# Moving the second output unit's split behind the scan, and the gate copy one head later

## The chip, the cores and the metric

The kernel is one program on one core of a Trainium2 chip. It works in float32 on a sequence of 256 tokens of width 1024. The metric is the device time of one execution in microseconds; of several executions the median is taken.

The engines named below are TensorE (PE in the profile, with PEld for its weight loads), VectorE (DVE), ScalarE (ACT), GpSimd (POOL) and SyncE (SP), whose queue issues the weight transfers.

## What is computed

The reference chains two blocks: two transformer layers, then a hybrid block of two gated MLPs with a mixer between them. The change lies in the mixer, which runs a latent attention (8 heads) and a state-space scan (16 heads) over one input projection and multiplies both results by one output matrix:

```python
def hybrid_mixer(h, positions, w_in, ...):
    proj = h @ w_in
    z, xs, Bm, Cm, dt_raw, cq, ckv, k_rope_raw = jnp.split(proj, IN_SPLITS, axis=-1)
    ...
    y = ssd_chunked(xh, dt, A, Bm, Cm)
    y = y + d_skip * xh
    yg = (y.reshape(b, S, D_SSD) * jax.nn.silu(z)).reshape(b, S, SSD_GROUPS, D_SSD // SSD_GROUPS)
    y_ssd = rmsnorm(yg, ssd_norm_w)
    ...
    attn = mla_causal_attention(q_nope, q_rope, k_nope, k_rope, v)
    y_mla = rmsnorm(attn, mla_norm_w)
    return jnp.concatenate([y_ssd, y_mla], axis=-1) @ w_out
```

## The kernel before

**Weight units.** All weights come in units of 1 MB (128 x 2048 numbers), through a ring of three slots. A unit takes three steps. SP loads it into `raw` (line 421 issues it). ACT copies it, rounded to the matmul's number format, into `whi` (line 593). DVE subtracts, `wlo = raw - whi` (line 1039). These two steps together are "the split" of a unit, and PE then multiplies by both parts, three matmuls for each product. Units are split strictly in order: `splits(n)` on ACT and on DVE does all units up to n that are still to do, and `w_hi`, `w_lo` and `w_used` count what ACT, DVE and PE have done. Three rules tie the ring together:

- SP loads unit n once DVE has split unit n - 3.
- ACT splits unit n once it has landed and PE has used unit n - 3.
- PE starts unit n once DVE has split it.

**The place.** The mixer's last input units are U_Z to U_Z+3, which give the gate z; its output units are U_OUT to U_OUT+7. U_OUT to U_OUT+3 multiply the latent attention's result (`bh`, `bl`), and U_OUT+4 to U_OUT+7 the scan's (`ah`, `al`). The order of everything is written out by hand, one in-order program for each engine. Around the change it is:

1. Split of U_OUT on ACT and on DVE.
2. The 8 latent heads (`mla_heads` on each engine). For head h PE computes the scores (`mla_score`, lines 2034, 2035 and 2020). DVE takes the row maximum (`head_max`, lines 1134, 1135 and 1138). ACT takes the exponential (`head_exp`, lines 716 and 718). PE transposes the weights (`weights_T`, line 1911). ACT copies them out of PSUM (`p_copy`, line 725). PE multiplies by the values (`values`, lines 1928 to 1930). PE's order in the loop is transposes of head h, scores of head h+2, values of head h-1.
3. The scan's preparation, and its 16 heads: PE lines 2336 to 2359, ACT lines 988 and 989, DVE line 1713.
4. `splits(U_OUT + 2)`, the silu of the second half of z, the sums y (lines 1706 and 1707), their norm (lines 1052 to 1058 and 1731), and `splits(U_OUT + 4)`. PE meanwhile runs U_OUT to U_OUT+2, then transposes the normed sums (line 1881), then runs U_OUT+3 and the rest.

**Inside step 2**, three pieces stand on DVE between the maxima that are no part of the heads. Behind head 1's maximum come the split of U_OUT+1 and the copy of half of z out of PSUM (line 1199; it waits on `z_half`, which PE signals ahead of the first transposes, and PE's values of heads 4 and on wait for it, since they reuse its two banks). Behind head 3's maximum comes `gate_diag` (line 1446). On ACT the split of U_OUT+1 stands between the exponential of head 1 and the copy of head 0's transposed weights.

Of the kernel before, what the change touches and what calls it, by code (L numbers as in the profile page):

```python
# [64 lines left out]
U_OUT = U_Z + 4  # L65
# [43 lines left out]
def build(nc, t_in, out):  # L109
    g = t_in  # L110
    with ExitStack() as ctx:
# [239 lines left out]
        def slot(n):  # L351
            return n % RING
# [4 lines left out]
        def bank(b, n=512):  # L357
            return ps[:, b, 0:n]
# [31 lines left out]
        def unit_size(n):  # L390
            if U_TAIL <= n < U_TAIL + 4:
                return 2 * TAILW
            if n == U_UQ + 1:
                return 768
            if n in (U_UQ, *U_KV):
                return 2 * 768
            return UNIT
# [186 lines left out]
        def _(act):  # L584
# [3 lines left out]
            def split(n, s, size=UNIT):  # L588

                act.wait_ge(w_landed[s], landed(n, s))  # L590
                if not isinstance(n, int) or n >= RING:
                    act.wait_ge(w_used, used(n))
                A.activation(whi[:, s, 0:size], raw[:, s, 0:size], ACT.Copy).then_inc(w_hi, 1)  # L593
# [13 lines left out]
            def splits(upto):  # L607
                while done[0] <= upto:
                    split(done[0], slot(done[0]), unit_size(done[0]))
                    done[0] += 1  # L610
# [100 lines left out]
            def head_exp(hg, h, src, scale):  # L711
                act.wait_ge(maxed, hg + 1)
                if h >= 2:
                    act.wait_ge(p_tr, hg - 1)
                b = h % 2
                A.activation(pb[:, b, 0:P], src(b)[:, 0:P], ACT.Exp, bias=nmx[:, b, 0:1], scale=scale,  # L716
                             accum_out=rs[:, 0, h:h + 1])
                A.activation(pb[:, b, P:SEG], src(b)[:, P:SEG], ACT.Exp, bias=nmx[:, b, 1:2], scale=scale,
                             accum_out=rs[:, 1, h:h + 1]).then_inc(exped, 1)

            def p_copy(hg, h):
                act.wait_ge(p_tr, hg + 1)
                if h >= 2:
                    act.wait_ge(pv_done, hg - 1)
                A.activation(pt[:, h % 2], bank(2 + h % 2, SEG), ACT.Copy).then_inc(p_copied, 1)
# [7 lines left out]
            def mla_heads(h0, scale):  # L733
                for h in range(HM):
                    head_exp(h0 + h, h, lambda b: bank(b, SEG), scale)
                    if h == 1:
                        splits(U_OUT + 1)
                    if h:
                        p_copy(h0 + h - 1, h - 1)
                p_copy(h0 + HM - 1, HM - 1)  # L740
# [224 lines left out]
            ins.then_inc(mqk_copied, 1)  # L965
            splits(U_OUT)
            mla_heads(2 * H, QK ** -0.5)

            for k, (lo, hi) in enumerate(O_PARTS):
# [52 lines left out]
        def _(dve):  # L1022
# [10 lines left out]
            def split(u, s, size=UNIT):  # L1033

                if isinstance(u, int):
                    dve.wait_ge(w_hi, u + 1)
                else:
                    dve.wait_ge(w_hi, u[1] * 6 + (u[0] + 1))
                V.tensor_tensor(wlo[:, s, 0:size], raw[:, s, 0:size], whi[:, s, 0:size].bitcast(F32),  # L1039
                                ALU.subtract).then_inc(w_lo, 1)  # L1040

            def splits(upto):
                while done[0] <= upto:
                    split(done[0], slot(done[0]), unit_size(done[0]))
                    done[0] += 1
# [85 lines left out]
            def head_max(hg, h, src, scale):  # L1131

                b = h % 2
                V.reduce_max(mx[:, b, 0:1], src[:, 0:P], AX_X)
                link(V.reduce_max(mx[:, b, 1:2], src[:, P:SEG], AX_X))
                if h >= 2:
                    dve.wait_ge(exped, hg - 1)
                V.tensor_scalar(nmx[:, b], mx[:, b], -scale, None, ALU.mult).then_inc(maxed, 1)  # L1138

            def o_part(h0, lo, hi):  # L1140

                dve.wait_ge(exped, h0 + hi)
                link(V.reciprocal(rinv[:, :, lo:hi], rs[:, :, lo:hi]))
                dve.wait_ge(pv_done, h0 + hi)
                half, n = lo // (HM // 2), (hi - lo) * VH
                src = lambda t: ps[:, 7, t * VH:t * VH + VH] if hi == HM else ps[:, 6 - 2 * half + t, 0:n]
                for t in range(TT):
                    V.tensor_tensor(xn[:, t, lo * VH:hi * VH].rearrange("p (h n) -> p h n", n=VH),
                                    src(t).rearrange("p (h n) -> p h n", n=VH),
                                    rinv[:, t, lo:hi].unsqueeze(2).to_broadcast([P, hi - lo, VH]),  # L1150
                                    ALU.mult).then_inc(o_ready, 1)
# [40 lines left out]
            def mla_heads(h0, scale):  # L1192
                for h in range(HM):
                    dve.wait_ge(scored, h0 + h + 1)
                    head_max(h0 + h, h, bank(h % 2, SEG), scale)
                    if h == 1:
                        splits(U_OUT + 1)
                        dve.wait_ge(z_half, 1)
                        V.tensor_copy(z[:, :, 512:D], ps[:, 4:6]).then_inc(z_raw, 1)
                    if h == 3:  # L1200
                        gate_diag(1, mix_diag)
                    if h >= HM - 2:
                        o_part(h0, *O_PARTS[h - HM + 2])
                o_part(h0, *O_PARTS[2])
# [239 lines left out]
            def gate_diag(k, dst=diag):  # L1444

                V.tensor_tensor(dst, ident[:].unsqueeze(1).to_broadcast([P, CT, P]),
                                modT[:, k, 2 * CT:3 * CT].unsqueeze(2).to_broadcast([P, CT, P]),
                                ALU.mult).then_inc(diag_done, 1)
# [231 lines left out]
            link(ins)  # L1680
            splits(U_OUT)
            mla_heads(2 * H, QK ** -0.5)

            dve.wait_ge(ac_ps, 1)
# [716 lines left out]
```

## Time and profile before

| | us |
|---|---|
| median of 3 runs | 1236.24 |
| lowest and highest of them | 1235.91 and 1247.31 |
| profiled execution, its own time | 1238.66 |
| its span in the trace | 1237.0 |

| engine | busy us | share of the span |
|---|---|---|
| PE | 1201.1 | 97% |
| DVE | 828.4 | 67% |
| ACT | 597.9 | 48% |
| POOL | 70.4 | 6% |

The page gives for each engine the time it was busy, and the chain of work that ended last, followed back from the last instruction. Of that chain PE has 90%, DVE 5%, ACT 3%, "issue" 1% and DMA 0%. PEclk is the clock that TensorE was granted, as a share of full speed. A row of the timeline begins with an instruction's start and its duration, both in us from the span's start; in square brackets stands how long its engine had been idle before it, and who ended that wait. Starts on one engine can lie closer together than the durations say, since an instruction's end overlaps the start of the next.

### The profile page before, as it was taken

How to read it: one execution, taken by the hardware profiler on the slowest of the kernel's cores; microseconds unless marked ns; L12 is line 12 of the kernel's file. 1: busy time of each engine (PE TensorE's matmuls, PEld its weight loads, DVE VectorE, ACT ScalarE, POOL GpSimd, SP SyncE). 2: the span in 40 equal slices, each digit the busy share in tenths (PEclk: the TensorE clock that was granted, in tenths of full speed). 3: DMA queues.
4: the chain of work that ended last, by engine and by line, in shares of the span. 5: the costliest groups of instructions: out<-in, count | busy, mean ns of one | idle time of the engine just before them, and what ended most of it. 6: DMA issues, size and time to landing. Idle time of an engine off the chain costs nothing.

```text
span 1237.0 us, 19961 instructions
## 1 busy us (share of the span) xinstructions
PE 1201.1 (97%) x7963; PEld 1091.9 (88%) x7963; DVE 828.4 (67%) x1113; ACT 597.9 (48%) x789; POOL 70.4 (6%) x106
## 2 busy tenths in 40 slices
PE   8999999999999999999999999999998999999997
PEld 7897899999888889999979999998987888999996
DVE  6676777777766769777665654547985866554445
ACT  5545543444545554444365344446746745443433
POOL 9100011110000001111000000000000000000000
PEclk9999999999999999999999999999998999999999
DMA  7633699888363259888544555544561043565560
GB/s 247 220 132 109 211 334 306 302 288 280 113 205 125 81 204 337 287 290 301 178 137 170 188 188 183 176 155 161 187 205 69 1 170 115 195 201 172 175 213 35
DMA packets 143240, 236.38 MB, mean 191 GB/s; under 512 B 6357, under 2 KB 106950, under 8 KB 143174
## 3 DMA queue, kind: packets, MB, share of 16 engines
q1 hardware_dynamic: 130402, 196.73, 47.7%
q0 software_dynamic: 10400, 37.77, 8.6%
q10 hardware_dynamic: 2372, 0.96, 0.3%
q8 instruction: 46, 0.75, 0.3%
q14 instruction: 20, 0.16, 0.0%
HBM read 234.37 MB, written 1.05 MB: 190 GB/s over the span
## 4 chain that ended last, share of the span: by engine, by line
PE 90%; DVE 5%; ACT 3%; issue 1%; DMA 0%; DVEq 0%; ACTq 0%
PE ps L1782 13%; PE ps L1784 13%; PE ps L1783 13%; PE ps L1857 10%; PE ps L1859 10%; PE ps L1861 10%; PE ps L1794 2%; PE ps L1796 2%; PE ps L1795 2%; PE ps L1946 1%; PE ps L2043 1%; PE ps L1948 1%; PE ps L1947 1%; PE ps L2028 1%; PE ps L1821 1%
## 5 line engine op out<-in xcount | busy, mean ns | idle before, releaser
L1039 DVE TENSOR_TENSOR wlo<-raw,whi 128x2048 fp32r<-128x2048 f32 (+2 forms) x187 | 421.4, 2259 | 187.2 <-ACT whi L593 186.7
L593 ACT ACTIVATE whi<-raw 128x2048 fp32r<-128x2048 f32 (+2 forms) x187 | 352.6, 1888 | 246.5 <-PE ps L1861 146.5
L1782 PE MATMUL ps<-ah,whi 128*128 128x256 f32 x1392 | 396.1, 285 | 9.9 <-DVE al L1102 3.8
L1783 PE MATMUL ps<-al,whi 128*128 128x256 f32 x1392 | 394.5, 283 | 0.0
L1784 PE MATMUL ps<-ah,wlo 128*128 128x256 f32 x1392 | 394.5, 283 | 0.0
L1782 PEld LDWEIGHTS ps<-ah,whi 128*128 128x128 f32 x1392 | 267.6, 192 | 14.5 <-issue 6.9
L1783 PEld LDWEIGHTS ps<-al,whi 128*128 128x128 f32 x1392 | 267.6, 192 | 1.8
L1784 PEld LDWEIGHTS ps<-ah,wlo 128*128 128x128 f32 x1392 | 267.6, 192 | 0.0
L1857 PE MATMUL ps<-whi,hh 128*128 128x512 f32 x376 | 117.2, 393 | 0.0
L1859 PE MATMUL ps<-wlo,hh 128*128 128x512 f32 x376 | 116.3, 390 | 0.0
L1861 PE MATMUL ps<-whi,hl 128*128 128x512 f32 x376 | 115.9, 389 | 0.0
L1859 PEld LDWEIGHTS ps<-wlo,hh 128*128 128x128 f32 x376 | 70.6, 188 | 15.2
L1861 PEld LDWEIGHTS ps<-whi,hl 128*128 128x128 f32 x376 | 70.6, 188 | 15.2
L1428 DVE SCALAR_TENSOR_TENSOR stage<-stage,cact 128x1024 f32<-128x1024 f32 x63 | 80.7, 1281 | 1.4
L1857 PEld LDWEIGHTS ps<-whi,hh 128*128 128x128 f32 x376 | 67.5, 189 | 11.2
L804 ACT ACTIVATE work<-ps 128x512 f32<-128x512 f32 x32 | 19.2, 598 | 115.3 <-PE ps L1784 115.3
L566 POOL DMA_DIRECT2D stage<-in_w_ada_dram x72 | 38.3, 532 | 445.2 <-PE ps L1981 154.6
L800 ACT ACTIVATE work<-ps 128x512 f32<-128x512 f32 x22 | 13.2, 599 | 87.9 <-PE ps L1784 87.9
L1375 DVE TENSOR_TENSOR hl<-work,hh 128x512 fp32r<-128x512 f32 x54 | 37.4, 692 | 18.1 <-ACT hh L802 16.9
L1370 DVE TENSOR_TENSOR work<-work,ps 128x512 f32<-128x512 f32 x22 | 15.1, 687 | 50.9 <-ACT work L800 50.9
L716 ACT ACTIVATE work<-ps,nmx 128x128 f32<-128x128 f32 x40 | 14.7, 368 | 63.8 <-DVE nmx L1138 63.8
L1857 PE MATMUL ps<-whi,ah 128*128 128x512 f32 x120 | 37.3, 381 | 0.0
(392 smaller groups left out, 1666.3 us busy)
## 6 DMA issues: line engine op xcount, KB each, us to landing
stage<-in_w_ada_dram POOLq DMA_DIRECT2D x72, 512.0 KB, 6.6
raw<-in_w_up_dram SPq DMA_DIRECT2D x32, 1024.0 KB, 6.9
raw<-in_w_down_dram SPq DMA_DIRECT2D x32, 1024.0 KB, 7.6
raw<-in_ffn_w_gate_dram SPq DMA_DIRECT2D x22, 1024.0 KB, 5.1
raw<-in_ffn_w_up_dram SPq DMA_DIRECT2D x22, 1024.0 KB, 5.1
raw<-in_ffn_w_down_dram SPq DMA_DIRECT2D x22, 1024.0 KB, 5.0
raw<-in_moba_w_qkv_dram SPq DMA_DIRECT2D x11, 1024.0 KB, 7.0
raw<-in_w_in_dram SPq DMA_DIRECT2D x10, 1024.0 KB, 5.0
```

What stands on the lines that cost most here:

```text
L566: pool.dma_start(aslot[:, c % ADA_RING], ada[:, c, bass.ds(b * D, D)]).then_inc(a_landed[c % ADA_RING], 16)
L593: A.activation(whi[:, s, 0:size], raw[:, s, 0:size], ACT.Copy).then_inc(w_hi, 1)
L1039: V.tensor_tensor(wlo[:, s, 0:size], raw[:, s, 0:size], whi[:, s, 0:size].bitcast(F32), ALU.subtract).then_inc(w_lo, 1)
L1375: V.tensor_tensor(flat(hl[:, buf]), hs, flat(hh[:, buf]).bitcast(F32), ALU.subtract).then_inc(h_ready, 1)
L1428: V.scalar_tensor_tensor(aacc, v, cact[:, c:c + 1], aacc, ALU.mult, ALU.add).then_inc(a_sum, 1)
L1782: T.matmul(o, wmh, xh[:, c], start=(c == 0), stop=False)
L1783: T.matmul(o, wmh, xl[:, c], start=False, stop=False)
L1784: ins = T.matmul(o, wml, xh[:, c], start=False, stop=(c == CT - 1))
L1794: T.matmul(o, wmh, xh[:, c], start=(c == 0), stop=False)
L1857: T.matmul(o, xh[:, c, tt], wh[:, k, v:e], start=(first and k == 0), stop=False)
L1859: T.matmul(o, xh[:, c, tt], wl[:, k, v:e], start=False, stop=False)
L1861: ins = T.matmul(o, xl[:, c, tt], wh[:, k, v:e], start=False, stop=(last and k == kn - 1))
```

## The change

The split of U_OUT+1 leaves the latent heads on both engines. It is now done by the call `splits(U_OUT + 2)` that stands behind the scan's 16 heads and so does two units there instead of one. The copy of the half of z moves from behind head 1's maximum to behind head 2's. The first piece of the diff is ACT's program, the second DVE's.

```diff
             def mla_heads(h0, scale):
                 for h in range(HM):
                     head_exp(h0 + h, h, lambda b: bank(b, SEG), scale)
-                    if h == 1:
-                        splits(U_OUT + 1)
                     if h:
                         p_copy(h0 + h - 1, h - 1)
...
                 for h in range(HM):
                     dve.wait_ge(scored, h0 + h + 1)
                     head_max(h0 + h, h, bank(h % 2, SEG), scale)
-                    if h == 1:
-                        splits(U_OUT + 1)
+                    if h == 2:
                         dve.wait_ge(z_half, 1)
                         V.tensor_copy(z[:, :, 512:D], ps[:, 4:6]).then_inc(z_raw, 1)
                     if h == 3:
```

The lines behind the edits move up by two in ScalarE's part and by three from VectorE's loop on, so that DVE's line 1039 becomes 1037, 1134 becomes 1132, and 1199 becomes 1196.

DVE in the latent heads, before, from the maximum of head 1 to the maximum of head 4's first row (1134, 1135 and 1138 are one head's maximum, 1039 a split, 1199 the copy of z, 1446 the gate's diagonal):

```order
L1134 TENSOR_REDUCE mx<-ps 128x1
L1135 TENSOR_REDUCE mx<-ps 128x1
L1138 TENSOR_SCALAR nmx<-mx 128x2
L1039 TENSOR_TENSOR wlo<-raw,whi 128x2048
L1199 COPY stage<-ps 128x2x512
L1134 TENSOR_REDUCE mx<-ps 128x1
L1135 TENSOR_REDUCE mx<-ps 128x1
L1138 TENSOR_SCALAR nmx<-mx 128x2
L1134 TENSOR_REDUCE mx<-ps 128x1
L1135 TENSOR_REDUCE mx<-ps 128x1
L1138 TENSOR_SCALAR nmx<-mx 128x2
L1446 TENSOR_TENSOR stage<-ident,modT 128x1024
```

The same stretch of DVE after the change:

```order
L1132 TENSOR_REDUCE mx<-ps 128x1
L1133 TENSOR_REDUCE mx<-ps 128x1
L1136 TENSOR_SCALAR nmx<-mx 128x2
L1132 TENSOR_REDUCE mx<-ps 128x1
L1133 TENSOR_REDUCE mx<-ps 128x1
L1136 TENSOR_SCALAR nmx<-mx 128x2
L1196 COPY stage<-ps 128x2x512
L1132 TENSOR_REDUCE mx<-ps 128x1
L1133 TENSOR_REDUCE mx<-ps 128x1
L1136 TENSOR_SCALAR nmx<-mx 128x2
L1443 TENSOR_TENSOR stage<-ident,modT 128x1024
```

Head 2's maximum now follows head 1's at once; the copy stands between heads 2 and 3, and the split is gone.

DVE behind the scan, before, from the last three heads' products (1713) to the sums y (1706 and 1707):

```order
L1713 TENSOR_TENSOR work<-work,stage 128x384 x3
L1039 TENSOR_TENSOR wlo<-raw,whi 128x2048
L1706 TENSOR_TENSOR stage<-stage,ps 128x512
L1707 TENSOR_TENSOR stage<-stage 128x512
L1706 TENSOR_TENSOR stage<-stage,ps 128x512
L1707 TENSOR_TENSOR stage<-stage 128x512
```

And after:

```order
L1710 TENSOR_TENSOR work<-work,stage 128x384 x3
L1037 TENSOR_TENSOR wlo<-raw,whi 128x2048 x2
L1703 TENSOR_TENSOR stage<-stage,ps 128x512
L1704 TENSOR_TENSOR stage<-stage 128x512
L1703 TENSOR_TENSOR stage<-stage,ps 128x512
L1704 TENSOR_TENSOR stage<-stage 128x512
```

Two splits now stand ahead of the sums instead of one. ACT's program has the same two moves: one split fewer behind head 1's exponential, and two in a row instead of one behind the scan's last exponential. The rows of PE, SP and POOL stay in their order.

## Rows read from the trace of the kernel before

**Rows 1.** Chain of work that ended last, 925 to 1055 us: start, us, what

```profile
937.96 1.81 ACT whi L593
939.80 0.23 DVE wlo L1039
...
944.95 0.90 PE ps L1911 x3
```

**Rows 2.** Timeline of DVE in the latent heads: start, us, what, idle before

```profile
939.80 2.29 DVE L1039 TENSOR_TENSOR wlo<-raw,whi 128x2048 fp32r<-128x2048 f32 x1 [2.81 <-ACT whi L593]
942.01 1.22 DVE L1199 COPY stage<-ps 128x1024 f32<-128x1024 f32 x1
943.14 0.28 DVE L1134 TENSOR_REDUCE mx<-ps 128x1 f32<-128x128 f32 x1
...
943.86 0.28 DVE L1134 TENSOR_REDUCE mx<-ps 128x1 f32<-128x128 f32 x1
...
944.59 1.22 DVE L1446 TENSOR_TENSOR stage<-ident,modT 128x1024 f32<-128x1024 f32 x1
...
952.85 0.29 DVE L1134 TENSOR_REDUCE mx<-ps 128x1 f32<-128x128 f32 x1 [1.23 <-PE ps L2020]
```

**Rows 3.** Timeline of ACT in the same stretch

```profile
939.64 0.50 ACT L725 ACTIVATE work<-ps 128x384 f32<-128x384 f32 x1
943.99 0.37 ACT L716 ACTIVATE work<-ps,nmx 128x128 f32<-128x128 f32 x1 [3.84 <-DVE nmx L1138]
```

**Rows 4.** Timeline of PE in the same stretch

```profile
938.69 0.49 PE L1911 MATMUL ps<-ident,work 128*128 128x128 f32 x3
...
939.48 0.47 PE L2020 MATMUL ps<-maskq,identr 128*128 128x256 f32 x1
...
940.59 0.47 PE L2020 MATMUL ps<-maskq,identr 128*128 128x256 f32 x1
...
941.34 0.39 PE L1930 MATMUL ps<-stage,work 128*128 128x128 f32 x2
944.95 0.90 PE L1911 MATMUL ps<-ident,work 128*128 128x128 f32 x3 [3.23 <-ACT work L718]
...
951.55 0.49 PE L1911 MATMUL ps<-ident,work 128*128 128x128 f32 x3
...
952.35 0.47 PE L2020 MATMUL ps<-maskq,identr 128*128 128x256 f32 x1
...
953.32 0.49 PE L1911 MATMUL ps<-ident,work 128*128 128x128 f32 x3
```

**Rows 5.** Windows of 4 us: length, busy of PE, PEld, DVE, ACT, POOL, PEclk, DMA

```profile
944.00:948.00 4.00, 3.05 (x13) 2.86 (x14) 2.38 (x6) 2.47 (x10) 0.00 (x0) 0.55 0.60 244
948.00:952.00 4.00, 4.00 (x22) 3.81 (x22) 0.97 (x5) 1.75 (x7) 0.00 (x0) 0.60 0.00 0
...
980.00:984.00 4.00, 3.27 (x26) 2.99 (x25) 3.81 (x8) 2.20 (x6) 0.00 (x0) 1.00 0.02 4
```

**Rows 6.** Timeline behind the scan, rows of DVE, of ACT and of PE

```profile
986.79 2.29 DVE L1039 TENSOR_TENSOR wlo<-raw,whi 128x2048 fp32r<-128x2048 f32 x1 [1.25 <-ACT whi L593]
...
995.76 1.67 DVE L1731 TENSOR_SCALAR stage<-stage,newt 128x512 f32<-128x512 f32 x4
...
1004.91 3.22 DVE L1098 SCALAR_TENSOR_TENSOR al<-ps,vA,ah 128x256 fp32r<-128x256 f32 x8 [3.08 <-ACT ah L634]
...
984.84 1.91 ACT L593 ACTIVATE whi<-raw 128x2048 fp32r<-128x2048 f32 x1
...
997.55 1.92 ACT L593 ACTIVATE whi<-raw 128x2048 fp32r<-128x2048 f32 x1 [2.41 <-PE ps L1861]
...
991.86 0.61 PE L1857 MATMUL ps<-whi,bh 128*128 128x512 f32 x2
...
1002.74 1.91 PE L1881 MATMUL ps<-ident,stage 128*128 128x128 f32 x16
```

**Rows 7.** DMA issues, 915 to 1060 us: KB each, median us to landing

```profile
raw<-in_w_out_dram SPq DMA_DIRECT2D x7, 1024.0 KB, 4.9
```

## The prediction

> **What bounds the kernel now.** The page comes first: PE is busy for 97% of the span and has 90% of the chain that ended last, so only a stretch in which PE stands still, or runs at the lower clock, can give time back. The chain says where that is near the change. In the latent heads it leaves PE, runs through ACT's copy of unit U_OUT+1 and DVE's subtraction, and returns to PE with the transposes of head 2's weights at 944.95 [rows 1]. In between lie the copy of z and head 2's maximum on DVE and its exponential on ACT.
>
> Then the timelines of the three engines. PE's row at 944.95 carries the idle time, 3.23 us, ended by ACT's exponential [rows 4]. ACT waited 3.84 us for head 2's maximum before that exponential [rows 3]. DVE did not begin the maximum until 943.14, behind the split (939.80) and the copy (942.01) [rows 2], though PE had finished head 2's scores at 939.48 + 0.47 = 939.95 [rows 4]. So the maximum was 3.2 us late, held by two pieces of work that no head needs.
>
> Last the windows, for the clock. From 944 to 952 the granted clock is 0.55 and 0.60 of full speed, which is mostly the lower level, 1.2 GHz [rows 5]; it fell while PE stood still for those 3.2 us. What it cost shows in the spacing of the transposes (T below, with the head's number): from T2 at 944.95 to T5 at 953.32 are 8.37 us for three heads, where the one step inside the full clock, T4 at 951.55 to T5, takes 1.77 us [rows 4].
>
> **The change in the heads.** I lay out the changed order with distances from the rows. All of them except PE's step lie on DVE and ACT, whose durations don't follow TensorE's clock:
>
> - a maximum starts 0.03 us behind the end of its scores (952.35 + 0.47 = 952.82 to 952.85) [rows 2, 4];
> - from its start to the start of the exponential are 0.85 us (943.14 to 943.99), and from there to T 0.96 us (943.99 to 944.95) [rows 2 to 4];
> - a maximum keeps DVE for 0.72 us (943.14 to 943.86), the copy for 1.13 us (942.01 to 943.14). The gate's diagonal has the copy's duration, 1.22 us, and gets the same 1.13 us [rows 2];
> - at full clock PE's scores end 1.27 us behind T (951.55 to 952.82), and the next T can follow 1.77 us behind it [rows 4].
>
> PE's past is unchanged up to the values of head 0, which end at 941.34 + 0.39 = 941.73 [rows 4]. I take PE as free for T2 then. Now:
>
> - Head 2: maximum 939.98, exponential 940.83, T2 allowed at 941.79. PE is free at 941.73, so **T2 is at 941.79**, 3.16 us earlier than before.
> - Head 3: its scores end at 940.59 + 0.47 = 941.06 [rows 4], but the copy of z now stands ahead of its maximum: 939.98 + 0.72 + 1.13 = 941.83. T3 is allowed at 943.64; PE, free at 941.79 + 1.77 = 943.56, waits 0.08 us.
> - Head 4: behind head 3's maximum (free at 942.55) comes the diagonal, so its maximum is at 943.68, where its scores ended at 943.06. T4 is allowed at 945.49; PE, free at 943.64 + 1.77 = 945.41, waits 0.08 us.
> - Head 5: scores end at 943.64 + 1.27 = 944.91, maximum 944.94. ACT comes to its exponential behind that of head 4 (944.53, some 0.9 us) and one copy of 0.50 us [rows 3], at about 945.9, so T5 is allowed at 946.9. PE is free at 945.49 + 1.77 = **947.26, which is T5**.
>
> T5 was at 953.32, so 6.06 us are gained. 3.16 of them are the stall. The other 2.90 are three heads at full clock (5.47 us instead of 8.37). From T5 on both kernels run the same instructions at the same distances, the waits of head 7 and of the scan included, and I carry the 6.1 us through unchanged.
>
> The copy of z keeps no cost of its own. Its signal `z_half` comes ahead of T0 (938.69), it would end near 941.9, and PE's first wait on it, the values of head 4, is behind T5. Queued behind it on DVE are heads 3 and 4, and the two waits of 0.08 us are that cost. If the cover were thinner by the copy's whole 1.13 us, that would be the price.
>
> **The change behind the scan.** Here one split is added on ACT (1.91 us) and one on DVE (2.29 us) [rows 6]. I cost both at nothing, and give the cover for each, in the old kernel's times:
>
> - *PE's unit U_OUT+1.* It starts at 991.86. Its split now takes the place of U_OUT+2's: ACT at 984.84, DVE at 986.79, done at 989.08 [rows 6]. Cover 2.8 us; at the least PE does not wait, at the most 2.29 us if the cover were gone.
> - *The sums and their norm.* These stand behind both splits on DVE. Their last row ends at 995.76 + 1.67 = 997.43; 2.29 later is 999.72. PE's transposes of them start at 1002.74 [rows 6], behind U_OUT to U_OUT+2. Cover 3.0 us. ACT's silu of z, later by 1.91, comes no later than DVE does.
> - *The next splits on DVE.* U_OUT+3 and U_OUT+4 come directly behind, about 4.5 us for two, now ending near 1004.2, where DVE's next work starts at 1004.91 [rows 6]. Cover 0.7 us, the thinnest; but the work behind it, 3.22 us, then ends at 1008.1, and PE wants it only behind U_OUT+3. A unit takes (1002.74 - 991.86) / 2 = 5.44 us, so that is not before 1009.9: another 1.8 us.
> - *The loads.* SP may load U_OUT+4 only once U_OUT+1 is split. That was at 942.1 and is now at 989.1 by the old times. With 4.9 us to landing [rows 7] it is there at 994.0; ACT, which waits for PE there anyway, takes it at 997.55 [rows 6]. Cover 3.5 us. The loads of U_OUT+5 and on are queued behind it on SP, each later by 2.3 us or less.
>
> **Sum.** 3.16 + 2.90 + 0 = 6.06 us, taken from the profiled execution's own 1238.66 us (span 1237.0 us): 1232.6 us. That execution stands 2.4 us above the median 1236.24 us. Against the median the sum gives 1230.2 us, my forecast.
>
> **The rivals.**
>
> *The clock falls all the same.* PE still waits at T3 and T4, and before that has a head's worth of light work. If the clock falls to 1.2 GHz during the heads, T2 to T5 takes the old 8.37 us and only the 3.16 us of the stall are gained: 1233.1 us. Against it: in 980 to 984 PE was busy for 3.27 of 4 us, with waits between heads, and the clock stayed at 1.00 [rows 5]; my schedule leaves less idle time than that. The Trainium skill ("TensorE: Matmul & The Clock Gate", "A second HAM failure mode: psum-queue depth-cycling") says that frequent short idles between groups of matmuls can make the clock swing; by that rule the outcome is this rival's, and this trace, with its clock of 1.00 in that window, does not bear it out. 15%.
>
> *Another wait takes the split's place.* If the maximum of head 2 is held by something the profile hides behind the split (ACT's copy of head 0's weights, PE's order), T2 stays near 944.95 and nothing is gained: 1236.2 us. Against it: the scores were ready at 939.95, and DVE's rows show no gap between split, copy and maximum. 7%.
>
> *More than the sum.* The values of head 0 waited for ACT's copy at 939.64 [rows 3], which stood behind ACT's split; with it gone, and the later waits of heads 6 and 7 shorter than they were, another 1 to 2 us could come: 1228.7 us. 7%.
>
> *Slower: the late load.* U_OUT+4 is loaded 47 us later than before, into a time when PE will need it. By the splits' durations (1.91 + 2.29 us), and with 0.8 us for the first of DVE's next rows, it must land by about 1004.9 to be ready for PE at 1009.9. That is 15.8 us after its issue, three times the 4.9 us of the row. Only a landing after 15.8 + 6.1 = 21.9 us makes the kernel slower than before, and each us beyond adds one; two of them give 1238.2 us. Nothing in the rows has such a landing. 3%.
>
> **How the numbers follow.** The forecast has 68%. The range runs from 1228.0, below the "more" case, to 1237.0, which takes in the fallen clock and the case of no gain with some scatter; what lies outside is below 2 in 10. The likeliest case alone spans 1229 to 1231.5. A measurement of this kernel can tell about 1%, that is 12.4 us, from no change. Only a gain of twice my sum would pass it, 2%; a loss that large would need a transfer over 30 us late or a disturbed measurement, 3%; within 1%, 95%.
>
> **What would show it.** Right: PE's idle time of 3.23 us before head 2's transposes shrinks below 0.3 us; the spacing of the transposes is 1.8 us from T2 on; PEclk is 1.00 from 940 to 956; the scan's heads start 6 us earlier; DVE shows two splits in a row behind the scan, and PE no wait before U_OUT+1, before the transposes of the sums, or before U_OUT+4. Wrong: a clock below 1 in the heads (then the 2.90 us are missing), or an idle PE in the 25 us behind the scan, with DVE's `wlo` or the norm named as the releaser.

## The result and the profile after

| | us |
|---|---|
| kernel before, median of 20 executions | 1237.04 (1234.17 to 1247.51) |
| changed kernel, median of 20 executions | 1232.49 (1231.84 to 1233.27) |
| ratio, 95% interval | 0.994 (0.992 to 0.9961) |
| profiled execution before, its time and span | 1238.66 and 1237.0 |
| profiled execution after, its time and span | 1232.97 and 1231.3 |

The changed kernel is faster by 4.55 us in the medians and by 5.69 us from one profiled execution to the other. The ratio shows more than the medians do (0.994 is 7.4 us). It goes with a tail of the kernel before: 6 of its 20 executions took 1245 to 1248 us, and none of the changed kernel's did, so the means lie 6.7 us apart (1239.2 and 1232.6).

The chain of work that ended last, of the changed kernel: start, us, what. ACT's and DVE's split are gone from it, and PE's transposes of head 2 come at 941.47 [rows 1].

```profile
940.96 0.46 ACT work L718 x2
941.47 0.55 PE ps L1908 x3
```

The timeline of DVE in the latent heads, changed kernel: start, us, what, and idle time before. Head 2's maximum starts at 939.64 and waits for PE's scores; the copy of z (line 1196) and the diagonal (line 1443) stand behind the maxima of heads 2 and 3 [rows 2].

```profile
939.64 0.29 DVE L1132 TENSOR_REDUCE mx<-ps 128x1 f32<-128x128 f32 x1 [3.00 <-PE ps L2017]
...
940.38 1.22 DVE L1196 COPY stage<-ps 128x1024 f32<-128x1024 f32 x1
941.51 0.28 DVE L1132 TENSOR_REDUCE mx<-ps 128x1 f32<-128x128 f32 x1
...
942.23 1.22 DVE L1443 TENSOR_TENSOR stage<-ident,modT 128x1024 f32<-128x1024 f32 x1
```

The timeline of ACT there. The first copy of the transposed weights starts at 938.86, as soon as PE has them; the exponential of head 2 waits 1.15 us instead of 3.84 us [rows 3].

```profile
938.86 0.49 ACT L725 ACTIVATE work<-ps 128x384 f32<-128x384 f32 x1 [1.25 <-PE ps L1908]
940.50 0.37 ACT L716 ACTIVATE work<-ps,nmx 128x128 f32<-128x128 f32 x1 [1.15 <-DVE nmx L1136]
```

The timeline of PE, the transposes of heads 0, 2, 3, 4, 5 and 7. From head 2 to head 5 none carries an idle time, where head 2's carried 3.23 us before [rows 4].

```profile
938.34 0.49 PE L1908 MATMUL ps<-ident,work 128*128 128x128 f32 x3
...
941.47 0.55 PE L1908 MATMUL ps<-ident,work 128*128 128x128 f32 x3
...
943.33 0.55 PE L1908 MATMUL ps<-ident,work 128*128 128x128 f32 x3
...
945.19 0.55 PE L1908 MATMUL ps<-ident,work 128*128 128x128 f32 x3
...
947.02 0.49 PE L1908 MATMUL ps<-ident,work 128*128 128x128 f32 x3
...
950.54 0.55 PE L1908 MATMUL ps<-ident,work 128*128 128x128 f32 x3 [0.59 <-ACT work L718]
```

The windows: length, busy time of PE, PEld, DVE, ACT and POOL, PEclk, DMA. The granted clock is 1.00 through the heads, where it was 0.55 and 0.60 [rows 5]. In this trace it falls once, later, at the start of the last MLP (1032 to 1040 us).

```profile
944.00:948.00 4.00, 4.00 (x32) 3.79 (x31) 2.34 (x9) 3.18 (x13) 0.00 (x0) 1.00 0.01 2
948.00:952.00 4.00, 3.41 (x29) 3.15 (x28) 1.63 (x7) 2.88 (x10) 0.00 (x0) 1.00 0.00 0
...
1032.00:1036.00 4.00, 2.56 (x13) 2.39 (x14) 3.67 (x8) 3.58 (x8) 0.00 (x0) 0.80 0.00 0
1036.00:1040.00 4.00, 4.00 (x29) 4.00 (x28) 2.92 (x3) 3.98 (x4) 0.00 (x0) 0.78 0.00 0
```

The timeline behind the scan, rows of DVE and of PE. DVE does two splits in a row from 980.50; the norm of the sums ends at 991.44 + 1.68 = 993.12, and PE's transposes of them start at 996.47 without a wait [rows 6].

```profile
980.50 4.49 DVE L1037 TENSOR_TENSOR wlo<-raw,whi 128x2048 fp32r<-128x2048 f32 x2 [1.24 <-ACT whi L593]
...
991.44 1.68 DVE L1728 TENSOR_SCALAR stage<-stage,newt 128x512 f32<-128x512 f32 x4
993.03 4.49 DVE L1037 TENSOR_TENSOR wlo<-raw,whi 128x2048 fp32r<-128x2048 f32 x2
998.63 3.23 DVE L1096 SCALAR_TENSOR_TENSOR al<-ps,vA,ah 128x256 fp32r<-128x256 f32 x8 [1.12 <-ACT ah L634]
```

```profile
996.47 1.91 PE L1878 MATMUL ps<-ident,stage 128*128 128x128 f32 x16
```

The loads of the output units take 4.8 us to landing (median of 7), where it was 4.9 us before [rows 7].

### The profile page after: what moved, and what is told of

It is laid out like the page before. It is cut to its first block, busy times and chain, and to the rows that moved or that the text cites. A ratio compares the mean times of both kernels' runs of the same rounds, so it can differ in the third digit from the quotient of the medians.

```text
span 1231.3 us, 19961 instructions
## 1 busy us (share of the span) xinstructions
PE 1198.8 (97%) x7963; PEld 1089.7 (89%) x7963; DVE 828.4 (67%) x1113; ACT 597.7 (49%) x789; POOL 70.5 (6%) x106
## 4 chain that ended last, share of the span: by engine, by line
PE 91%; DVE 4%; ACT 3%; issue 1%; DMA 0%; ACTq 0%; DVEq 0%
PE ps L1779 14%; PE ps L1781 13%; PE ps L1780 13%; PE ps L1854 10%; PE ps L1856 10%; PE ps L1858 10%; PE ps L1791 2%; PE ps L1793 2%; PE ps L1792 2%; PE ps L1943 1%; PE ps L2040 1%; PE ps L1945 1%; PE ps L1944 1%; PE ps L2025 1%; PE ps L1818 1%
```

## Where the time went, from trace to trace

I cut both traces at PE's transposes of head 0 and of head 7:

| stretch | before | after | difference |
|---|---|---|---|
| start to head 0's transposes | 938.69 | 938.34 | -0.35 |
| head 0's to head 7's transposes | 18.14 | 12.20 | -5.94 |
| head 7's transposes to the end | 280.2 | 280.8 | +0.6 |

The heads give 5.94 us. The 0.6 us behind them are lost where the clock fell at the start of the last MLP in this trace and not in the one before. The -0.35 us ahead of the heads is no gain of the change either: the trace of the kernel before had a fall of the clock at the start of the hybrid block's first MLP (650 to 655 us, PEclk 0.66), and this one has none there. The stretch behind the scan gave none of it: from head 7's transposes to those of the sums it is 45.91 us before (956.83 to 1002.74) and 45.93 us after (950.54 to 996.47).

## Experiments

The runs were taken in four jobs, the last three on a chip of their own each, and the kernel before ran in every one. The table has for each kernel the spacing of PE's transposes in its trace, counted from head 0's, and its median with the number of executions. Beside the 1237.04 us of the first job, the medians of the kernel before were 1236.22 us (35) in the job of e1 to e4, 1236.01 us (29) in that of e5 to e7, and 1238.22 us (25) in that of e8 to e10. So the same kernel's median moves by 2.2 us from job to job, and the gain of the same change is 4.55 us in the first job and 1238.22 - 1231.99 = 6.23 us in the last.

| kernel | to head 2 | to head 5 | to head 7 | median us |
|---|---|---|---|---|
| before | 6.26 | 14.63 | 18.14 | |
| before, second trace | 6.27 | 13.29 | 16.81 | 1235.43 (1) |
| changed | 3.13 | 8.68 | 12.20 | 1232.49 (20) |
| e1, e9 split alone (spacing of e1) | 3.15 | 8.53 | 12.04 | 1231.81 (12), 1231.70 (11) |
| e2 copy alone | 5.13 | 12.12 | 15.64 | 1235.20 (12) |
| e3 PE kept busy | 6.27 | 11.65 | 15.17 | 1234.90 (12) |
| e4 split in head 4 | 3.13 | 12.66 | 18.05 | 1237.82 (12) |
| e5, e10 division moved (spacing of e5) | 3.16 | 8.54 | 11.67 | 1231.10 (12), 1231.31 (9) |
| e6 one split more | 3.13 | 8.68 | 12.20 | 1231.93 (10) |
| e7 two splits more | 3.13 | 8.68 | 12.19 | 1234.19 (10) |
| e8 changed, again | 3.13 | 8.67 | 12.19 | 1231.99 (12) |

### Which of the two moves carries the gain

Split alone: the changed kernel with the copy of z back behind head 1's maximum.

```diff
-                    if h == 2:
+                    if h == 1:
                         dve.wait_ge(z_half, 1)
                         V.tensor_copy(z[:, :, 512:D], ps[:, 4:6]).then_inc(z_raw, 1)
```

> Only the split of U_OUT+1 is moved behind the scan; the copy of z stays behind head 1's maximum. Theory (the split was the stall): the copy waits for z_half, which in the trace of the changed kernel comes near 938.3 us, so it runs from about 938.6 to 939.7 us and is over when head 2's scores are ready at 939.6 us. Head 2's transposes stay within 0.2 us of the changed kernel's 941.47 us, head 3's maximum is free about 1.1 us sooner but PE is the pace there, so the time is that of the changed kernel, 1232.5 us, within 0.5 us. Rival (the copy's move carries part of the gain): the copy in front of head 2's maximum costs its whole 1.13 us, 1233.6 us.

Measured: 1231.81 us, ratio to before 0.9951 (0.9928 to 0.9973). Head 2's transposes come 3.15 us behind head 0's, as in the changed kernel (3.13), and head 5's come 0.15 us sooner (8.53 against 8.68). The copy is hidden on either side of head 2's maximum; the rival's 1.13 us is not there. Moving the split is the whole gain; moving the copy adds nothing to it.

Copy alone: the kernel before with only the copy moved.

```diff
                     if h == 1:
                         splits(U_OUT + 1)
+                    if h == 2:
                         dve.wait_ge(z_half, 1)
```

> Only the copy of z is moved behind head 2's maximum; the split stays in the heads. Theory (the sum is in the order of the work): head 2's maximum follows the split at once, at about 942.0 instead of 943.14 us, and the transposes of head 2 come at 943.8 instead of 944.95 us. If the clock still falls while PE stands idle for some 2.1 us, the gain over the kernel before is 1.1 us (1235.9 against 1237.0 us); if it does not fall, 1.1 + 2.9 = 4.0 us (1233.0 us). The granted clock between 944 and 952 us says which. Rival (the copy alone is what matters): all of the gain, 1232.5 us, with the split still in place.

Measured: 1235.20 us (1232.98 to 1236.46), ratio 0.9973 (0.995 to 0.9995). The wait of PE before head 2's transposes shrinks from 3.23 to 2.10 us, by the copy's 1.13 us, and the clock still falls, though for less than before. The timeline and the windows of this kernel:

```profile
943.04 0.90 PE L1912 MATMUL ps<-ident,work 128*128 128x128 f32 x3 [2.10 <-ACT work L718]
```

```profile
940.00:944.00 4.00, 1.90 (x13) 1.71 (x12) 3.93 (x9) 1.36 (x6) 0.00 (x0) 0.88 0.42 104
944.00:948.00 4.00, 4.00 (x23) 3.77 (x23) 2.03 (x5) 2.52 (x10) 0.00 (x0) 0.69 0.39 162
948.00:952.00 4.00, 4.00 (x34) 3.90 (x34) 2.95 (x11) 2.59 (x10) 0.00 (x0) 1.00 0.01 2
```

From head 2 to head 5 it takes 6.99 us, between the 5.4 of full clock and the 8.37 of the first trace. Expected had been one or the other. The 12 executions fall in two groups, five at 1233.0 to 1233.9 us and seven at 1235.1 to 1236.5 us. The trace (1235.34 us) is of the second group; that the first group's clock stayed up in the heads would fit their time, but no trace shows it.

### Is the clock a term of its own

The kernel before, with its stall, and PE given 24 transposes in the stall that nothing needs (their bank is overwritten by head 2's).

```diff
                     if h:
                         values(h - 1)
+                    if h == 1:
+                        for _ in range(24):
+                            T.transpose(ps[:, 2, 0:P], ident[:], ident[:])
```

> The kernel before with its stall untouched, but with 24 transposes of the identity added on PE behind the values of head 0, into the PSUM bank that head 2's transposes overwrite; they take some 2.7 us (16 such transposes take 1.75 us) of the 3.2 us in which PE stood idle. Theory (the clock is a term of its own, 2.9 us): head 2's transposes stay at 944.95 us, the clock stays at 1.00 from 944 to 952 us, and from head 2's to head 5's transposes it takes 5.5 instead of 8.4 us, so 2.9 us are gained: 1234.1 against 1237.0 us. Rival (the slow spacing of heads 2 to 4 comes from DVE and ACT, not from the clock): spacing 8.4 us as before, 1237.0 us.

Measured: 1234.90 us, ratio 0.997 (0.9944 to 0.9996). The timeline of PE, and the windows:

```profile
940.13 2.78 PE L1940 MATMUL ps<-ident 128*128 128x128 f32 x24
943.52 0.55 PE L1911 MATMUL ps<-ident,work 128*128 128x128 f32 x3 [0.61 <-ACT work L718]
```

```profile
940.00:944.00 4.00, 3.39 (x31) 3.15 (x30) 3.93 (x9) 1.45 (x7) 0.00 (x0) 1.00 0.56 168
944.00:948.00 4.00, 4.00 (x34) 3.87 (x32) 1.96 (x7) 2.81 (x13) 0.00 (x0) 1.00 0.24 96
```

Head 2's transposes are as late as before (6.27 us behind head 0's), the clock stays at 1.00, and from there to head 5's it takes 5.38 us instead of 8.37. The rival, that DVE and ACT set the slow spacing, is out. Against the first trace the clock term is 2.99 us. The medians of the job show only 1.3 us (1236.22 against 1234.90, and the interval of the ratio ends just below 1): the executions of the kernel before don't all pay that much, as the second trace of it shows.

### Two traces of the same kernel

> The kernel before, unchanged, for a second trace of it. Its executions fall in groups: 1234.2 to 1234.9 us at a mean clock of 0.997 to 0.998, 1235.8 to 1236.4 us at 0.997, 1237.6 to 1238.3 us at 0.993 to 0.995, and 1245.1 to 1247.3 us at 0.984 to 0.987. Theory (the groups differ by how long the clock stays low in and behind the latent heads): in a trace of another group than the first one's (0.993, 1238.66 us) the wait of PE before head 2's transposes is 3.2 us again, and the spacing from there to head 5's transposes differs from 8.4 us by about the difference in time. Rival (the groups differ elsewhere in the kernel): the same spacing of 8.4 us, and another stretch longer or shorter.

Measured: 1235.43 us, 3.23 us less than in the first trace. The timeline of PE and the windows of this second trace of the kernel before:

```profile
943.10 0.55 PE L1911 MATMUL ps<-ident,work 128*128 128x128 f32 x3 [3.23 <-ACT work L718]
...
945.32 0.85 PE L1911 MATMUL ps<-ident,work 128*128 128x128 f32 x3
948.35 0.49 PE L1911 MATMUL ps<-ident,work 128*128 128x128 f32 x3
```

```profile
944.00:948.00 4.00, 4.00 (x20) 3.79 (x19) 1.09 (x5) 1.99 (x8) 0.00 (x0) 0.57 0.11 44
948.00:952.00 4.00, 4.00 (x34) 3.90 (x33) 2.77 (x9) 2.59 (x10) 0.00 (x0) 1.00 0.01 2
```

The wait is the same 3.23 us, but the clock is back at 1.00 from 948 on, where the first trace had 0.60 [rows 5], and from head 2 to head 5 it takes 7.02 us instead of 8.37. So 1.33 us of the 3.23 (18.14 against 16.81 to head 7) lie in the heads, as the theory says; 1.86 us lie ahead of them (head 0's transposes at 936.83 against 938.69), where the other theory looked. Rows of ACT, each once from the first trace and once from the second, say where they arose:

```profile
25.00 1.92 ACT L593 ACTIVATE whi<-raw 128x2048 fp32r<-128x2048 f32 x1 [3.25 <-PE ps L1784]
23.75 1.92 ACT L593 ACTIVATE whi<-raw 128x2048 fp32r<-128x2048 f32 x1 [2.73 <-PE ps L1784]
...
663.44 0.60 ACT L800 ACTIVATE work<-ps 128x512 f32<-128x512 f32 x1 [5.70 <-PE ps L1784]
661.55 0.60 ACT L800 ACTIVATE work<-ps 128x512 f32<-128x512 f32 x1 [5.08 <-PE ps L1784]
```

The first trace is 1.25 us late already at its 25th microsecond and 1.89 us late at its 663rd. In between it had the fall of the clock at 650 to 655 us, which the second trace lacks. So two thirds of the 1.86 us arose in the first 25 us of the kernel and 0.6 us at that fall.

### Does a split cost the same in another head

The changed kernel, with the split back among the heads, behind head 4 on both engines.

```diff
                 for h in range(HM):
                     head_exp(h0 + h, h, lambda b: bank(b, SEG), scale)
+                    if h == 4:
+                        splits(U_OUT + 1)
...
                     head_max(h0 + h, h, bank(h % 2, SEG), scale)
+                    if h == 4:
+                        splits(U_OUT + 1)
                     if h == 2:
```

> The changed kernel, with the split of U_OUT+1 put back among the latent heads, behind head 4's maximum on DVE and its exponential on ACT. Theory (a split anywhere among the heads stands on the chain, since ACT's and DVE's part follow each other): ACT's copy ends 1.9 us behind head 4's exponential, DVE's part 2.3 us later, and head 5's maximum comes near 949.3 instead of 944.7 us, so its transposes come some 4.1 us later than in the changed kernel: 1236.6 us, and up to 2.9 us more if the clock falls in the idle time, 1239.5 us. Rival (only head 2 was sensitive, later heads have slack): at most 1 us over the changed kernel, 1233.5 us.

Measured: 1237.82 us, ratio to before 1.0003 (0.9983 to 1.0024), inside the 1236.6 to 1239.5 us expected. The timeline, rows of ACT, DVE and PE, and the windows:

```profile
944.31 1.91 ACT L593 ACTIVATE whi<-raw 128x2048 fp32r<-128x2048 f32 x1
946.25 2.29 DVE L1039 TENSOR_TENSOR wlo<-raw,whi 128x2048 fp32r<-128x2048 f32 x1 [2.78 <-ACT whi L593]
948.46 0.29 DVE L1134 TENSOR_REDUCE mx<-ps 128x1 f32<-128x128 f32 x1
950.28 0.90 PE L1912 MATMUL ps<-ident,work 128*128 128x128 f32 x3 [2.70 <-ACT work L718]
```

```profile
948.00:952.00 4.00, 1.72 (x8) 1.63 (x8) 3.33 (x10) 2.48 (x10) 0.00 (x0) 0.64 0.59 176
952.00:956.00 4.00, 4.00 (x20) 3.91 (x19) 0.88 (x4) 1.41 (x5) 0.00 (x0) 0.51 0.21 86
```

The two halves of the split run one behind the other between head 4's maximum and head 5's, and head 5's transposes are 12.66 - 8.68 = 3.98 us later than in the changed kernel (4.1 expected). The clock falls with the wait of 2.70 us, and by head 7 it is 5.85 us. A split stands on the chain behind head 4 as it did behind head 1, and the rival of 1 us is out.

### How large is the cover behind the scan

DVE's half of the split done twice, for U_OUT+2 (e6), and for U_OUT+1 as well (e7). The second writes the same values. The diff is e7's; e6's has U_OUT+2 alone.

```diff
+                if isinstance(u, int) and u in (U_OUT + 1, U_OUT + 2):
+                    link(V.tensor_tensor(wlo[:, s, 0:size], raw[:, s, 0:size], whi[:, s, 0:size].bitcast(F32), ALU.subtract))
                 V.tensor_tensor(wlo[:, s, 0:size], raw[:, s, 0:size], whi[:, s, 0:size].bitcast(F32),
                                 ALU.subtract).then_inc(w_lo, 1)
```

> The changed kernel with DVE's half of the split of U_OUT+2 done twice behind the scan, some 2.4 us more on DVE ahead of the sums. The cover of the moved work is asked for. In the changed kernel's trace the norm of the sums ends at 993.12 us and PE's transposes of them start at 996.46 us, a cover of 3.3 us; DVE's next splits end at 997.5 us and the work behind them would start at 999.9 instead of 998.63 us and end at 1003.1 us, where PE comes to U_OUT+4 at 1003.67 us. Theory (covered): the time of the changed kernel, 1232.5 us, within 0.5 us. Rival (the stretch behind the scan is already at its limit, DVE paces it): 2.4 us longer, 1234.9 us.

Measured: 1231.93 us. A further 2.3 us on DVE behind the scan cost nothing against the changed kernel of another job (1232.49 us, and 1231.99 us in e8's), and PE shows no wait between the scan and U_OUT+4.

> The changed kernel with DVE's halves of the splits of U_OUT+1 and U_OUT+2 both done twice behind the scan, some 4.8 us more on DVE. Theory (cover of 3.3 us at the transposes of the sums): PE waits there for about 1.5 us, and the time is 1234.0 us. Rival 1 (DVE paces the stretch): 4.8 us longer, 1237.3 us. Rival 2 (the cover is larger than read, all hidden): 1232.5 us.

Measured: 1234.19 us, 1.7 us above the changed kernel's 1232.49 us and 2.3 us above e6 of the same job. The timeline of PE has two waits:

```profile
995.52 1.97 PE L1880 MATMUL ps<-ident,stage 128*128 128x128 f32 x16 [0.41 <-DVE stage L1730]
...
998.51 0.73 PE L1856 MATMUL ps<-whi,bh 128*128 128x512 f32 x2 [1.02 <-DVE wlo L1039]
```

Together they are 1.43 us, where 1.5 us were expected, all of it at the transposes. 1.02 us of it stand before U_OUT+3, whose split DVE does behind the norm. The idle times don't count all that was lost. From head 7's transposes to PE's first row of U_OUT+3 it takes 49.47 us here (949.04 to 998.51) and 47.59 us in the changed kernel (950.54 to 998.13), so PE comes there 1.88 us later, and from head 7's transposes to the end e7 takes 1.9 us more than e6. With 4.65 us more on DVE ahead of that split (it starts 47.14 us behind head 7's transposes, and 42.49 us in the changed kernel), the cover at this place was 4.65 - 1.88 = 2.8 us beyond what the change uses. The trace is of the fastest of e7's 10 executions (1232.75 us), with the clock at 1.00 at both MLPs, so the loss has to be read from these stretches and not from its time.

### A faster version

The split alone moved, and besides the first division of the heads' sums, which stood ahead of head 7's maximum, put behind it.

```diff
                     if h == 3:
                         gate_diag(1, mix_diag)
-                    if h >= HM - 2:
-                        o_part(h0, *O_PARTS[h - HM + 2])
+                    if h == HM - 1:
+                        o_part(h0, *O_PARTS[0])
+                        o_part(h0, *O_PARTS[1])
```

> A version meant to be the fastest: the split alone moved, as in e1 (copy of z behind head 1's maximum), and besides the first division of the heads' sums (line 1148 of the kernel before, 1.2 us on DVE) moved from in front of head 7's maximum to behind it. In the changed kernel's trace DVE reaches head 7's maximum at 948.72 us behind that division, while the scores end at 948.28 us, and PE then waits 0.59 us for head 7's exponential. Theory (that wait is on the chain): 0.4 us less than e1's 1231.8 us, 1231.4 us. Rival (the division is itself wanted soon, by ACT's squares and PE's values of head 7): nothing gained or up to 0.8 us lost, 1231.8 to 1232.6 us.

Measured: 1231.10 us (1230.35 to 1241.23). PE's wait before head 7's transposes goes from 0.59 to 0.20 us, in its timeline:

```profile
949.37 0.55 PE L1909 MATMUL ps<-ident,work 128*128 128x128 f32 x3 [0.20 <-ACT work L718]
```

To settle differences of under 1 us, the three versions ran again on one chip:

> The changed kernel itself, on one chip with the two versions below, since differences of under 1 us between jobs on different chips can't be told. Theory (position of the copy is worth 0.15 us, read from the spacing of the transposes: 8.68 us from head 0's to head 5's here, 8.53 us in e1): 0.1 to 0.2 us above the split-alone version. Rival (the 0.7 us between the medians 1232.49 and 1231.81 us belong to the copy's place): 0.7 us above it.

> The split-alone version of e1 again. Theory: 0.1 to 0.2 us below the changed kernel of the same job. Rival: 0.7 us below it.

> The version of e5 again (split alone, first division behind head 7's maximum). Theory: 0.4 us below the split-alone version of the same job, as its transposes of head 7 came 0.37 us sooner behind head 0's in the trace (11.67 against 12.04 us), so 0.5 us below the changed kernel. Rival (the 0.7 us below e1 in the other job was the chip): equal to the split-alone version.

Measured: 1231.99, 1231.70 and 1231.31 us. The copy's place is worth 0.3 us (0.15 us in the traces) and the division's 0.4 us (0.37 us in the traces); the ranges of the executions overlap, and what supports such small differences is that the traces give them too. Of each of the two gaps of 0.7 us between medians of different jobs (1232.49 to 1231.81, and 1231.81 to 1231.10), the rest goes with the job. e10 is the fastest of the versions, with one execution of 9 at 1239.86 us and, in e5, one of 12 at 1241.23 us.

## Why the prediction was right, point by point

**The stall.** Right, and to the size: 3.16 us forecast, 6.26 - 3.13 = 3.13 us measured. The row that the forecast rested on was PE's idle time with DVE's maximum behind it; e1 shows that the split was what held it.

**The clock.** Right as a mechanism: granted clock 1.00 through the heads, three heads in 5.55 us (5.47 forecast). e3 isolates it. The rival in which the clock falls all the same did not come; waits of up to 0.59 us in the heads left it at 1.00. The time alone would not have told them apart: 1232.49 us lies nearer to this rival's 1233.1 us than to the forecast of 1230.2 us. It is the trace that decides.

**The heads as a whole.** 6.06 us forecast, 5.94 us measured from head 0's to head 7's transposes. Heads 3 and 4 were followed by PE with hardly a gap, as laid out.

**The split behind the scan.** Right: PE waits nowhere there, and the stretch is 45.91 and 45.93 us long. The load of U_OUT+4, issued at 982.8, was covered; the rival of a late load had no part. One item was missing from the list of covers: PE wants U_OUT+3 directly behind the transposes of the sums, and its split stands behind the norm on DVE. It had some 2.8 us to spare (split done near 995.3, PE there at 998.13 us), and so the omission did no harm, but it was where e7 lost most.

**The number.** 1230.2 us forecast, 1232.49 us measured, inside the range, but 2.3 us too low. The step that failed is the last of the sum, "Against the median the sum gives 1230.2 us". It takes the clock's 2.90 us off the median, though they were read in one execution and the median does not contain them in full: the second trace of the same kernel paid 1.33 us less in the heads, and e3, which removes this price alone, gained 1.3 us in the medians. The stall's 3.13 us and these 1.3 us make 4.4 us; the split alone gained 4.41 us in that job (e1), and the changed kernel 4.55 us in the first. Against the sum's 6.06 us that is 1.5 us of the miss. The other 0.8 us lie in the starting point, a median of 3 executions (1236.24 us) that with 20 became 1237.04 us.

The sum against the profiled execution's own time gave 1232.6 us, close to what came, and part of that is luck. That execution was late for reasons outside the change as well, 1.25 us in its first 25 us and 0.6 us at the fall of the clock at 650 us, and the changed kernel's traces have delays of the same kind (head 0's transposes at 938.34 us in the first of them and at 936.85 us in e7's).

**The rival of "more than the sum".** It did not come, and one of its two readings was wrong. The values of head 0 did not wait for ACT's copy in the kernel before: they carry no idle time and start 2.20 us behind head 0's transposes both before (938.69 to 940.89) and after (938.34 to 940.54). The waits of head 7 stayed as they were (0.57 and 0.59 us).

**The chances.** The time stayed within 1%, as forecast with 95%. The prediction gives no weight to the execution of 1247.31 us among its three; such executions turned out to belong to the kernel before and so to the comparison.

## To carry to other kernels

Between two steps of a loop that three engines pass a tile around, a piece of work that two of them must do one behind the other costs both its parts and not the longer one, here 3 to 4 us for a split of 1.9 and 2.3 us; put it where the engine that waits for it has several units of its own work left. A stall of TensorE of a few us has a second price, the clock behind it, which can be as large as the stall. And where an expected gain contains such a clock price, read it in more than one execution, or measure it as e3 does, before you take it off a median: here one trace said 2.99 us and the medians 1.3 us.

## What the runs showed of the hardware

**The price of the same wait varies from execution to execution.** With PE idle for 3.23 us in both traces of the kernel before, the three heads behind it took 8.37 us in one and 7.02 us in the other; full clock is 5.38 us (e3). The clock also fell behind waits of 2.10 us (e2) and 2.70 us (e4), and not in the heads of kernels whose waits there were 0.61 us or less. The Trainium skill ("TensorE: Matmul & The Clock Gate", "What's actually happening") describes the clock gate's window as free-running, so that the moment of a change depends on where in it the work falls; two traces of one kernel with different prices for the same wait agree with that.

**A wait of 1.8 us can do it, and need not.** At the start of each of the hybrid block's two MLPs PE waits 1.7 to 1.8 us for DVE. The first of them in e1's trace and in the changed kernel's (PE's row, then the window around or behind it):

```profile
649.18 0.55 PE L1779 MATMUL ps<-ah,whi 128*128 128x256 f32 x1 [1.80 <-DVE al L1100]
648.00:652.00 4.00, 2.82 (x13) 2.85 (x14) 3.78 (x8) 3.59 (x7) 0.00 (x0) 0.58 0.00 0
...
650.13 0.36 PE L1779 MATMUL ps<-ah,whi 128*128 128x256 f32 x1 [1.79 <-DVE al L1100]
652.00:656.00 4.00, 3.65 (x28) 3.36 (x28) 3.32 (x4) 4.00 (x4) 0.00 (x0) 1.00 0.00 0
```

In e1 the clock falls there; in the changed kernel's trace it falls at the second of these places instead (1032 to 1040 us). Of the 13 traces of all versions, eight have the fall at the first place, two at the second, and three at neither. Between the two traces of the kernel before, one with it and one without, it made 0.6 us. The moved work does not stand at either place, so these 0.6 us are scatter in every comparison above; why the fall comes now at one place, now at the other or at none was not tested.

**The kernel before has a tail.** Over four sets of executions 27 of 109 took 1243 us or more, in e1's job at a mean granted clock of 0.984 to 0.987 against 0.993 to 0.998 in the others. Of all other versions together, 2 of 132 took over 1239 us, both of the version with the moved division. So removing, shortening or moving the stall, or keeping PE busy in it, went together with the loss of the tail. No trace fell on such an execution, so where in it the clock stayed low was not seen, and the cause stays open.
